# Routed experts: from adding rows in memory to writing one row per assignment and summing at the end

## The chip, the cores and the metric

One core of a Trainium2 chip runs the kernel. The metric is the device time of an execution in microseconds. A core has TensorE (PE, with its weight loads PEld), VectorE (DVE), ScalarE (ACT), GpSimd (POOL) and SyncE (SP), which run side by side and wait for one another by semaphores, and 16 DMA engines for transfers between memory and the core's own buffers.

## The reference, cut to what matters

One layer of a decoder: 512 tokens of 1024 values, float32. A mixing part (pooling, windowed attention, gates) comes first, then a mixture of experts, then a gated projection of a second input. The part at issue is the mixture:

```
x = x + merged @ w_out                                   # 512 x 1024
h2 = rmsnorm(x, g_ffn)
idx, w = route(h2, ...)                                  # 8 of 64 experts for each token, 8 weights
moe = sum over the 8: w * ((silu(h2 @ w_gate[e]) * (h2 @ w_up[e])) @ w_down[e])     # hidden width 256
x = x + moe + swiglu(h2, w_sh_gate, w_sh_up, w_sh_down)  # the shared expert
x = x + sigmoid(rmsnorm(x, g_ple) @ w_ple_gate) * rmsnorm(p @ w_ple_proj, g_ple_post)
```

512 tokens with 8 experts each are 4096 assignments, 64 for each expert on average.

## The kernel before

The kernel is one hand-ordered program: each engine has its list of instructions, and semaphores join them. Tokens are worked on in four tiles of 128 (`NT = 4`). Weights come through a ring of 12 slots of 1 MB, loaded on SyncE's queue in a written order.

**The head.** x and the input weights are loaded, ScalarE squares the rows, and then stores tile 0 of x to 128 spare "dump" rows of the accumulator in memory (L577), which only have to hold something finite. The mixing part follows. VectorE then computes the routing (L927 to L989): group scores, the best eight experts of each token, the weights, and a table `tokcol` of six columns per token and expert. TensorE counts each token's place in its expert's list (the rank product, L1469 to L1472, behind the shared expert's L1428), VectorE makes 0/1 matrices out of the places (L1002), and small products with `tokcol` (L1456) give, for each expert, a list of up to 96 tokens with their weights. VectorE turns it into row numbers (L1037 to L1046): `slot_ix` holds the token's row, and empty places point at dump rows. Meanwhile the sum of x and the shared expert's output (L1443 and L1017) is stored by ScalarE's queue as the base of the accumulator, four stores of 512 KB (L652).

**The loop over experts.** One expert is a step, on 96 rows. GpSimd gathers the rows of `h2` with an indirect DMA (L487) three steps ahead, copying the row numbers to a small buffer first (L483). TensorE transposes them (L1180), multiplies by gate and up weights (L1504, 8 products, each in two passes), transposes the activations (L1512) and multiplies by the down weights (L1525, 4 products in two passes). ScalarE evacuates half of the transposes (L659), takes the Silu (L664) and weights the result (L669); VectorE does the other half of the transposes (L1053), the product with the up part (L1058) and the transposed activations (L1063). TensorE's order in step e is: gate and up of e, transposes of e-1's activations, transposes of e+1's rows, down of e-1. GpSimd then issues an indirect DMA that adds the 96 weighted rows to the accumulator in memory (L498). Two experts may hold the same token, so each such write waits until the last has landed:

```python
pool.wait_ge(added, 16 * e)
pool.wait_ge(y_ready, e + 1)
ticket(1, ticket_done[1])
pool.indirect_dma_start(acc, ..., yrow[j][0:CAP, :], None, compute_op=ALU.add).then_inc(added, 16)
```

The row buffers `yrow` are four, so ScalarE's weighting waits for the write of four steps back. SyncE loads the three weight units of the expert four steps on, as its slots become free (L365). Further rounds for lists of more than 96 tokens exist, and are skipped with these inputs' lists.

**The tail.** When all writes have landed, GpSimd sets a marker (L564) and ScalarE's queue loads the four tiles of the accumulator back to `xrow` (L721). For each tile: ScalarE squares (L724), GpSimd takes the root (L435, L436), VectorE scales (L1137), TensorE transposes (L1180), VectorE copies with the gains (L1143), TensorE multiplies by the gate weights in two halves of 32 passes each (L1624), ScalarE takes the sigmoid (L731), VectorE multiplies and adds (L1153, L1154) and SyncE stores (L407). All the transposes of tile i+1 stand before the gate products of tile i.

Of the kernel before, what the change touches and what calls it, by code (L numbers as in the profile page):

```python
# [7 lines left out]
ALU = mybir.AluOpType  # L8
# [6 lines left out]
P = 128  # L15
# [19 lines left out]
DUMP = T  # L35
ACC_ROWS = T + P
# [4 lines left out]
UNROLL = SLOTS // 3  # L41
AHEAD = UNROLL - 1
TURNS = NE // UNROLL
NVEC = 22
LCOL = 6
# [8 lines left out]
C_NDUMP = C_P + 1  # L54
C_IC = C_NDUMP + 1
# [3 lines left out]
def constant_table():  # L59
# [10 lines left out]
    c[:, C_NDUMP] = -(DUMP + p)  # L70
# [31 lines left out]
TAIL_SLOT = [9, 10, 11, 0]  # L102

# [9 lines left out]
def build(nc, t, acc, h2_dram, out):  # L113
    ctx = ExitStack()
    with ctx:
# [3 lines left out]
        def sem(name):  # L119
# [21 lines left out]
        slot_ix = sb("slot_ix", [P, NE], U32)  # L141
        slot_w = sb("slot_w", [P, NE])
        stage = sb("stage", [P, 2, UNROLL, 1], U32)
# [29 lines left out]
        pT = qa[:, 0:1024].rearrange("p (j n) -> p j n", j=2)  # L173
        r_sc, r_sel, r_w, r_rank = (qa[:, 1024 + k * NR:1024 + (k + 1) * NR] for k in range(4))
# [4 lines left out]
        rbias = ka[:, LM + NR // 2:LM + NR // 2 + NE]  # L179
        small = ka[:, LM + NR // 2 + NE:2 * T]  # L180

        o_place = poolbuf[:, 0:NT * CAP // 2].bitcast(BF16).rearrange("p (i r) -> p i r", i=NT)
        o_iota = sb("o_iota", [P, CAP])
        o_lst = sb("o_lst", [P, LCOL + 4])
        o_ix = sb("o_ix", [P, 1], U32)
# [4 lines left out]
        hg = [xrow[:, k, :] for k in range(UNROLL)]  # L190
        yrow = [rows[:, k, :] for k in range(UNROLL)]
        hgT = [lo[:, k * KD * CAP:(k + 1) * KD * CAP].rearrange("p (k n) -> p k n", k=KD) for k in range(2)]
        eactT = [lo[:, 1536 + k * 2 * CAP:1536 + (k + 1) * 2 * CAP].rearrange("p (j n) -> p j n", j=2)
                 for k in range(2)]
# [3 lines left out]
        lists_sb = rows[:, 0, 0:NE * LCOL].rearrange("p (e c) -> p e c", c=LCOL)  # L198
        ltmp = [rows[:, 0, 512 + k * NE:512 + (k + 1) * NE] for k in range(4)]
# [3 lines left out]
        def bank(b, n=1):  # L203
# [39 lines left out]
        shdown_ps, base_ready, base_stored = (  # L243
            sem("shdown_ps"), sem("base_ready"), [sem(f"base_stored{i}") for i in range(NT)])
        dump_stored = sem("dump_stored")
# [3 lines left out]
        gathered = [sem(f"gathered{j}") for j in range(UNROLL)]  # L249
# [55 lines left out]
        def further_rounds(eng, start, step):  # L305
# [6 lines left out]
            with eng.Fori(1, ROUNDS) as j:  # L312
                with eng.If(longest > j * CAP):
                    start(j)
                    with eng.Fori(0, NE) as e:
                        step(e, (j - 1) * NE + e, j)
# [1346 lines left out]
```

## Time and profile before

| | |
|---|---|
| median of 3 runs | 1256.97 us (1254.72 to 1257.39) |
| profiled execution, span | 1254.2 us (the execution's own time is not given beside it) |
| busy: TensorE, VectorE, ScalarE, GpSimd | 1205.2, 249.3, 203.5, 256.8 us |
| mean granted clock of TensorE | 0.986 |
| moved by DMA | 288.56 MB, 230 GB/s over the span |
| chain that ended last | TensorE 90%, "issue" 5%, DMA 3%, VectorE 1%, ScalarE 1% |

The span runs from the first to the last instruction. A busy time is the sum of an engine's instructions, whether or not anybody waited for them. The granted clock is a share of TensorE's full 2.4 GHz. The chain is followed back from the last instruction, at each step to what released it; only what stands in it sets the time.

### The profile page before, as it was taken

The page shows a single profiled execution, that of the slowest core. Times are in us where ns is not written, and L with a number is a line of the kernel's source. Part 1 is how long each engine was busy: PE and PEld are TensorE (multiplying, and loading weights), DVE is VectorE, ACT ScalarE, POOL GpSimd, SP SyncE. Part 2 cuts the span into 40 slices and gives each one's busy share as a digit, 9 for nine tenths or more (in the row PEclk, how much of TensorE's full clock was granted, in tenths as well). Part 3 has the DMA queues.
Part 4 walks back from the last instruction along what each step waited for, and adds up shares of the span by engine and source line. Part 5 has one row for each costly group of instructions (what it writes and reads, how often), then busy time and mean ns, then how long its engine had stood idle before and what let it go on. Part 6 is the DMA issues. An engine that isn't in the chain of part 4 may idle for free.

```text
span 1254.2 us, 11220 instructions
## 1 busy us (share of the span) xinstructions
PE 1205.2 (96%) x3867; PEld 583.5 (47%) x3867; DVE 249.3 (20%) x525; ACT 203.5 (16%) x356; POOL 256.8 (20%) x463
## 2 busy tenths in 40 slices
PE   6999999999999899999999999999999999999498
PEld 4644544444435544444444444444444444444287
DVE  3314520121248710111011101110111011101113
ACT  2003211300130011111111111111111111111210
POOL 3261000000010113223322332233223322332100
PEclk9999999999999899999999999999999999999799
DMA  9241212114131379999999999999999999998401
GB/s 332 72 152 51 67 58 76 67 67 177 39 145 40 152 270 339 332 333 334 336 326 337 336 337 330 335 339 335 325 336 333 338 328 331 338 335 244 111 1 67
DMA packets 72154, 288.56 MB, mean 230 GB/s; under 512 B 8556, under 2 KB 30592, under 8 KB 47168
## 3 DMA queue, kind: packets, MB, share of 16 engines
q1 hardware_dynamic: 55552, 239.15, 51.1%
q0 software_dynamic: 14704, 42.25, 14.4%
q10 hardware_dynamic: 1872, 6.82, 1.4%
q8 instruction: 17, 0.28, 0.1%
q14 instruction: 9, 0.07, 0.0%
HBM read 264.58 MB, written 31.98 MB: 236 GB/s over the span
## 4 chain that ended last, share of the span: by engine, by line
PE 90%; issue 5%; DMA 3%; DVE 1%; ACT 1%; POOL 0%; SPq 0%; POOLq 0%; DVEq 0%; ACTq 0%
PE ps L1504 35%; PE ps L1525 17%; PE ps L1259 9%; PE ps L1180 5%; PE ps L1624 4%; PE ps L1361 4%; PE ps L1203 2%; PE ps L1243 2%; PE ps L1346 2%; PE ps L1344 2%; PE ps L1398 1%; DMA ring<-in_w_in 1%; PE ps L1209 1%; PE ps L1512 1%; DMA accumulator<-rows,stage 1%
## 5 line engine op out<-in xcount | busy, mean ns | idle before, releaser
L1504 PE MATMUL ps<-ring,gates 128*96 128x512 f32 x1024 | 451.7, 594 | 1.5 <-ACT gates L659 1.5
L1504 PEld LDWEIGHTS ps<-ring,gates 128*96 128x96 f32 x1024 | 167.2, 163 | 274.5 <-issue 274.5
L1525 PE MATMUL ps<-ring,gates 128*96 128x512 f32 x512 | 230.4, 592 | 1.6 <-ACT rows L669 1.2
L1063 DVE COPY gates<-ps 128x192 f32<-128x192 f32 x64 | 22.9, 358 | 646.4 <-PE ps L1512 646.4
L1525 PEld LDWEIGHTS ps<-ring,gates 128*96 128x96 f32 x512 | 79.9, 166 | 104.2 <-issue 104.2
L478 POOL TENSOR_TENSOR tickets<-cst 128x1 f32<-128x1 f32 x125 | 23.7, 190 | 473.9 <-ACT rows L669 448.3
L1259 PE MATMUL ps<-actT,ring 128*128 128x512 f32 x256 | 112.3, 595 | 0.0
L669 ACT ACTIVATE rows<-ps,slot_w 96x1024 f32<-96x1024 f32 x64 | 71.1, 1110 | 200.7 <-DMA accumulator<-rows,stage 165.6
L498 POOL DMA_INDIRECT accumulator<-rows,stage x64 | 93.2, 1457 | 30.7 <-issue 30.7
L664 ACT ACTIVATE gates<-ps 96x256 f32<-96x256 f32 x64 | 24.3, 380 | 363.0 <-PE ps L1504 363.0
L1259 PEld LDWEIGHTS ps<-actT,ring 128*128 128x128 f32 x256 | 47.9, 190 | 59.6 <-issue 59.5
L487 POOL DMA_INDIRECT xrow<-h_rows,stage x64 | 65.7, 1027 | 35.1 <-issue 33.5
L435 POOL TENSOR_SCALAR st<-st 128x1 f32<-128x1 f32 (+1 forms) x20 | 6.6, 328 | 321.5 <-ACT rows L620 241.9
L1180 PE MATMUL ps<-cst,xrow 96*128 96x96 f32 x512 | 67.5, 275 | 3.1 <-DMA xrow<-h_rows,stage 3.1
L1180 PEld LDWEIGHTS ps<-cst,xrow 96*128 96x128 f32 x512 | 63.4, 211 | 4.4 <-issue 4.4
L483 POOL COPY stage<-slot_ix 128x1 uint32 (+1 forms) x128 | 50.7, 652 | 57.1 <-DVE slot_w L1046 53.9
L1361 PE MATMUL ps<-ring,gates 128*128 128x512 f32 x128 | 55.4, 593 | 2.1 <-DVE gates L875 2.1
L1624 PE MATMUL ps<-ring,actT 128*128 128x256 f32 x256 | 56.7, 383 | 0.0
L1624 PEld LDWEIGHTS ps<-ring,actT 128*128 128x128 f32 x256 | 49.2, 193 | 6.7
L1180 PE MATMUL ps<-cst,rows 128*128 128x128 f32 x96 | 16.5, 335 | 29.5 <-DVE rows L1137 16.1
L659 ACT ACTIVATE gates<-ps 128x384 f32<-128x384 f32 x64 | 31.4, 491 | 79.0 <-PE ps L1180 79.0
L1512 PEld LDWEIGHTS ps<-cst,gates 96*128 96x128 f32 x128 | 25.2, 197 | 31.8 <-issue 31.8
(178 smaller groups left out, 805.7 us busy)
## 6 DMA issues: line engine op xcount, KB each, us to landing
ring<-in_w_exp_gate SPq DMA_DIRECT2D x64, 1024.0 KB, 7.1
ring<-in_w_exp_up SPq DMA_DIRECT2D x64, 1024.0 KB, 11.3
ring<-in_w_exp_down SPq DMA_DIRECT2D x64, 1024.0 KB, 4.8
ring<-in_w_gate SPq DMA_DIRECT2D x8, 1024.0 KB, 9.6
ring<-in_w_in SPq DMA_DIRECT2D x5, 1024.0 KB, 14.3
ring<-in_w_out SPq DMA_DIRECT2D x4, 1024.0 KB, 4.9
ring<-in_w_ple_gate SPq DMA_DIRECT2D x4, 1024.0 KB, 12.4
accumulator<-xrow ACTq DMA_DIRECT2D x5, 512.0 KB, 4.6
```

The costliest lines, as they stand in the source:

```text
L483: nc.gpsimd.tensor_copy(stage[:, kind, j, :], slot_ix[:, bass.ds(e, 1)]).then_inc(staged, 1)
L487: pool.indirect_dma_start(hg[j][0:CAP, :], None, h2_dram, bass.IndirectOffsetOnAxis(ap=stage[0:CAP, 0, j, :], axis=0), bounds_check=T - 1, ...
L498: pool.indirect_dma_start(acc, bass.IndirectOffsetOnAxis(ap=stage[0:CAP, 1, j, :], axis=0), yrow[j][0:CAP, :], None, compute_op=ALU.add).t ...
L659: nc.scalar.activation(hgT[k][:, 4:8, :], bank(1)[:, 0:4 * CAP].rearrange("p (k n) -> p k n", k=4), ACT.Copy).then_inc(hgT_hi_ready, 1)
L669: nc.scalar.activation(yrow[j][0:CAP, :], bank(6, 2)[0:CAP, :], ACT.Copy, scale=slot_w[0:CAP, bass.ds(e, 1)]).then_inc(y_ready, 1)
L1180: last = nc.tensor.transpose(bank(b0 + half)[:, k * width:(k + 1) * width], v[0:width, 4 * half + k, :], ident[0:width, 0:width])
L1259: last = mm(bank(m % 2), w[:, k, (m % 2) * P:(m % 2 + 1) * P], actT[:, k, :], start=(k == 0), stop=(k == KD - 1))
L1361: last = mm(bank(half), gates[:, k, i * P:(i + 1) * P], w[:, k], start=(k == 0), stop=(k == KD - 1))
L1504: last = mm(bank(2 + k)[0:CAP, :], hgT[k][:, q, :], w[:, q], start=(q == 0), stop=(q == KD - 1))
L1512: last = nc.tensor.transpose(bank(4)[:, q * CAP:(q + 1) * CAP], v[:, q, :], ident[0:CAP, 0:CAP])
L1525: last = mm(bank(6 + half)[0:CAP, :], eactT[k][:, q, :], w[:, q, half * 512:(half + 1) * 512], start=(q == 0), stop=(q == 1))
L1624: last = mm(bank(half)[:, c * 256:(c + 1) * 256], actT[:, k, i * P:(i + 1) * P], w[:, k], start=(k == 0), stop=(k == KD - 1))
```

## The change

Each token gets eight rows of its own in memory (`y_dram`, 4096 rows of 4 KB, those of one token side by side), one for each of its eight experts. The routing also counts, for each token, the how-manieth of its experts an expert is (six more adds over shifted copies), and this number goes through the lists as a seventh column, so that each place of a list knows its own row: 8 x token + number. The expert loop writes its weighted rows there plainly; empty places get row number 4096, which the bounds check drops. Writes of different experts no longer wait for each other, only a row buffer waits for its own last write (one semaphore per buffer).

The base (x plus the shared expert) stays in `xrow` and is no longer stored; the store to the dump rows goes too. Gathered rows have moved to `actT`, with four buffers instead of three steps of lead. In the tail SyncE loads the eight rows of each token, four chunks of two rows (1 MB) per tile, into two buffers of four ring slots; VectorE adds them up and adds the sum to `xrow`. The transposes of the tail take `xrow` as it is, and the factor of the norm is applied as the scale of the sigmoid instead. TensorE's order in the tail is now: half a tile's gate product, the next tile's transposes, the other half.

```diff
-DUMP = T
-ACC_ROWS = T + P
+ACC_ROWS = T * TOPK
-LCOL = 6
+LCOL = 7
+Y_SLOT = [1, 5]
...
+        ysum = [ring[:, s:s + 4, :].rearrange("p u n -> p (u n)").rearrange("p (r n) -> p r n", r=TOPK)
+                for s in Y_SLOT]
...
+        y_rows = y_dram.rearrange("(i p r) n -> i p r n", p=P, r=TOPK)
...
             sp.wait_ge(ple_ps, NT)
             sp.wait_ge(shdown_ps, 2 * NT)
-            for b in base_stored:
-                sp.wait_ge(b, 16)
-            for g in gathered[:AHEAD]:
-                sp.wait_ge(g, 16)
             load_expert(3, 3, None)
...
-            sp.wait_ge(y_ps, NE - UNROLL + 1)
-            sp.wait_ge(gu_ps, NE - UNROLL + 2)
+            sp.wait_ge(gu_ps, (STEPS - 1))
+            sp.wait_ge(y_ps, (STEPS - 2))
             for c, s in enumerate(TAIL_SLOT):
                 sp.dma_start(unit_view(s, KD), ple_gate[:, :, c * 256:(c + 1) * 256]
                              ).then_inc(slot_loaded[s], 16)
+            sp.wait_ge(gu_ps, STEPS)
+            sp.wait_ge(y_ps, STEPS)
+            sp.wait_ge(experts_done, 1)
+            for i in range(NT):
+                if i >= 2:
+                    sp.wait_ge(x2_ready, i - 1)
+                for c in range(4):
+                    sp.dma_start(ysum[i % 2][:, 2 * c:2 * c + 2, :], y_rows[i][:, 2 * c:2 * c + 2, :]
+                                 ).then_inc(y_loaded[i % 2][c], 16)
...
+            def scatter(j):
+                pool.indirect_dma_start(y_dram, bass.IndirectOffsetOnAxis(ap=stage[0:CAP, 1, j, :], axis=0),
+                                        yrow[j][0:CAP, :], None, bounds_check=ACC_ROWS - 1, oob_is_err=False
+                                        ).then_inc(scattered[j], 16)
+            def move(r, j, before, first=False, last=False):
+                if not last:
+                    pool.wait_ge(hgT_ps, 2 * r + 2)
+                    stage_from(r + BUF, j)
...
+                    ticket(0, ticket_done[0])
+                    gather(j)
+                if before is not None:
+                    pool.wait_ge(scattered[j], 16 * before)
+                stage_to(r, j)
...
+                pool.wait_ge(y_ready, r + 1)
                 ticket(1, ticket_done[1])
+                scatter(j)
...
-            act.dma_start(acc[DUMP:DUMP + P, :], xrow[:, 0, :]).then_inc(dump_stored, 16)
...
-            for i in range(NT):
-                act.wait_ge(base_ready, 2 * i + 2)
-                act.dma_start(acc_rows[i], xrow[:, i, :]).then_inc(base_stored[i], 16)
...
-            for i in range(NT):
-                act.dma_start(xrow[:, i, :], acc_rows[i]).then_inc(x2_loaded[i], 16)
+            def sigmoid(i):
+                act.wait_ge(rstd3_ready, i + 1)
...
+                    nc.scalar.activation(sgate[i % 2][:, half * 512:(half + 1) * 512], bank(half), ACT.Sigmoid,
+                                         scale=st[:, 0, 8 + i:9 + i]).then_inc(sgate_ready, 1)
...
+            HEAD = NE // 2
+            for b in range(2):
+                nc.vector.memset(count_of[:, b, :, 0:HEAD], 0.0)
+            link(nc.vector.tensor_copy(count_of[:, 0, :, HEAD:], r_sel.rearrange("p (i e) -> p i e", i=NT)))
+            b, span = 0, 1
+            while span < NE:
+                link(nc.vector.tensor_tensor(count_of[:, 1 - b, :, HEAD:], count_of[:, b, :, HEAD:],
+                                             count_of[:, b, :, HEAD - span:HEAD - span + NE], ALU.add))
+                b, span = 1 - b, 2 * span
...
+            nc.vector.tensor_scalar(tokcol[:, :, :, 6], place_of, -1.0, None, ALU.add)
...
-            link(nc.vector.memset(slot_ix[:, :], DUMP))
-            link(nc.vector.tensor_tensor(slot_ix[0:CAP, :], a, b_, ALU.add))
+            link(nc.vector.tensor_tensor(row, a, b_, ALU.add))
+            nc.vector.tensor_copy(from_row[0:CAP, :], row)
+            nc.vector.scalar_tensor_tensor(to_row[0:CAP, :], row, float(TOPK), L[:, :, 6], ALU.mult, ALU.add)
...
+            def gather_sum(i, first):
+                y = ysum[i % 2]
+                turn = i // 2 + 1
+                if first:
+                    dve.wait_ge(y_loaded[i % 2][0], 16 * turn)
+                    dve.wait_ge(y_loaded[i % 2][1], 16 * turn)
+                    link(nc.vector.tensor_tensor(y[:, 0:2, :], y[:, 0:2, :], y[:, 2:4, :], ALU.add))
+                    return
+                for c in (2, 3):
+                    dve.wait_ge(y_loaded[i % 2][c], 16 * turn)
+                    link(nc.vector.tensor_tensor(y[:, 0:2, :], y[:, 0:2, :], y[:, 2 * c:2 * c + 2, :], ALU.add))
+                link(nc.vector.tensor_tensor(y[:, 0, :], y[:, 0, :], y[:, 1, :], ALU.add))
+                nc.vector.tensor_tensor(xrow[:, i, :], xrow[:, i, :], y[:, 0, :], ALU.add).then_inc(x2_ready, 1)
...
+            gather_sum(0, True)
+            gather_sum(0, False)
+            for i in range(NT):
+                if i + 1 < NT:
+                    gather_sum(i + 1, True)
+                third_T(i)
+                if i + 1 < NT:
+                    gather_sum(i + 1, False)
                 if i:
-                    third_T(i - 1)
-            third_T(NT - 1)
-            for i in range(NT):
-                result(i)
+                    result(i - 1)
+            result(NT - 1)
...
+            third_T(0)
+            for i in range(NT):
+                ple_gate_half(i, 0)
+                if i + 1 < NT:
+                    third_T(i + 1)
+                ple_gate_half(i, 1)
```

## Rows read from the trace of the kernel before

**Rows 1.** Chain of waits in the expert loop (start, length, what)
```profile
708.00 3.44 PE ps L1525 x8
711.43 6.87 PE ps L1504 x16
718.30 0.20 PE ps L1512 x2
718.50 0.89 PE ps L1180 x8
```

**Rows 2.** Busy time by stretch, loop: length, busy by engine, clock, DMA share, GB/s
```profile
700.00:800.00 100.00, 100.00 (x302) 44.42 (x301) 10.34 (x27) 17.83 (x27) 28.66 (x54) 1.00 0.96 334
```

**Rows 3.** Transfers of the whole kernel: issues, median us to landing
```profile
xrow<-h_rows,stage POOLq DMA_INDIRECT x64, 8.7
accumulator<-rows,stage POOLq DMA_INDIRECT x64, 9.8
```

**Rows 4.** Who waited for whom, 500 to 1100 us: total, times, longest
```profile
ACT rows L669 <- DMA accumulator<-rows,stage: 156.3, 50, 3.4
```

**Rows 5.** Chain of waits in the tail
```profile
1169.00 6.54 DMA accumulator<-rows,stage
...
1176.32 5.17 DMA accumulator<-rows,stage
...
1181.67 3.32 DMA xrow<-accumulator
...
1188.02 3.68 PE ps L1180 x16
...
1221.99 27.64 PE ps L1624 x128
```

**Rows 6.** Busy time by stretch, where the DMA engines are full, and one idle
```profile
8.00:12.00 4.00, 1.01 (x5) 1.02 (x6) 0.43 (x1) 2.30 (x4) 1.19 (x4) 1.00 1.05 375
405.00:407.00 2.00, 2.00 (x23) 1.41 (x22) 2.00 (x3) 0.00 (x0) 0.00 (x0) 1.00 0.97 406
1150.00:1155.00 5.00, 5.00 (x20) 2.60 (x19) 1.15 (x3) 0.87 (x2) 0.00 (x0) 1.00 1.03 275
1184.00:1186.00 2.00, 0.00 (x0) 0.00 (x0) 0.00 (x0) 0.99 (x2) 0.00 (x0) 0.50 1.06 367
1188.00:1190.00 2.00, 1.98 (x9) 1.98 (x10) 1.31 (x2) 1.18 (x3) 0.59 (x3) 0.50 0.29 119
```

**Rows 7.** Timeline of TensorE at the start (in brackets: idle before, releaser)
```profile
18.32 7.11 PE L1203 MATMUL ps<-ring,actT 128*128 128x512 f32 x16 [0.84 <-DMA ring<-in_w_in]
```

**Rows 8.** Timeline of VectorE in routing and lists
```profile
375.23 0.42 DVE L960 TENSOR_TENSOR gates<-gates,kT 128x256 f32<-128x256 f32 x1
...
381.33 0.72 DVE L980 CAST kT<-cst 128x256 bf16<-128x256 f32 x1 [0.69 <-issue]
...
387.77 0.42 DVE L991 SCALAR_TENSOR_TENSOR qT<-ps,qT 128x256 f32<-128x256 f32 x1 [2.52 <-PE ps L1472]
...
403.72 0.69 DVE L1010 TENSOR_TENSOR gates<-gates,ps 128x512 f32<-128x512 f32 x1 [1.34 <-ACT gates L647]
...
409.47 0.69 DVE L1017 TENSOR_TENSOR xrow<-xrow,ps 128x512 f32<-128x512 f32 x1 [0.82 <-PE ps L1443]
...
428.93 0.27 DVE L1041 SCALAR_TENSOR_TENSOR rows<-rows 96x64 f32<-96x64 f32 x1
```

**Rows 9.** Chain of waits at the entry into the expert loop
```profile
432.05 4.77 DMA xrow<-h_rows,stage
...
438.81 8.77 PE ps L1504 x16
```

**Rows 10.** Timeline of TensorE and SyncE's queue at the same place
```profile
428.16 5.66 PE L1443 MATMUL ps<-ring,gates 128*128 128x512 f32 x8
...
440.35 0.33 SPq L365 DMA_DIRECT2D ring<-in_w_exp_gate  x1
```

**Rows 11.** Timeline of ScalarE at the end of the loop
```profile
1172.07 1.11 ACT L669 ACTIVATE rows<-ps,slot_w 96x1024 f32<-96x1024 f32 x1 [3.89 <-PE ps L1525]
```

More of the change, by code:

```diff
@@ L501, in move @@
-            def move(e, j, first=False):
-                if not first:
-                    pool.wait_ge(hgT_ps, 2 * e)
-                stage_index(0, e + AHEAD, (j + AHEAD) % UNROLL)
-                stage_index(1, e + 1, (j + 1) % UNROLL)
-                if not first:
-                    pool.wait_ge(ticket_done[0], e)
-                pool.wait_ge(staged, 2 * e + AHEAD + 3)
-                ticket(0, ticket_done[0])
-                gather(e + AHEAD, (j + AHEAD) % UNROLL)
-                scatter(e, j, first)
+                scatter(j)
@@ L543, in o_start @@
+            for r in range(BODY):
+                move(r, r % BUF, r // BUF if r >= BUF else None, first=(r == 0))
+            with pool.Fori(1, TURNS - 1) as turn:
+                for j in range(BODY):
+                    move(turn * BODY + j, j % BUF, turn * (BODY // BUF) + j // BUF)
+            for r in range(STEPS - BODY, STEPS):
+                move(r, r % BUF, r // BUF, last=(r + BUF >= STEPS))
             def o_start(j):
-                pool.wait_ge(added, 16 * NE)
+                all_scattered(pool)
@@ L1530, in _ @@
             pe.wait_ge(base_ready, 2 * NT)
-            rows_T(0, 16, 0, None)
-            def static_uses(turn):
-                return lambda s: 16 * (USES[s] + turn + 1)
-            def step(e, j, uses, prev_uses, turn, g_next, first=False, second=False, last=False):
-                up(e, j, uses)
-                if not first:
-                    acts_T(e - 1, j - 1)
-                if not last:
-                    rows_T(e + 1, g_next, j + 1, 0)
-                if not first:
-                    down(e - 1, (j - 1) % UNROLL, prev_uses, first=second)
@@ L1563, in _, with static_uses, static_step @@
-            for e in range(NE - UNROLL, NE):
-                static_step(e)
-            acts_T(NE - 1, (NE - 1) % UNROLL)
-            down(NE - 1, (NE - 1) % UNROLL, static_uses(TURNS - 1))
+            def static_uses(group):
+                return lambda slot: 16 * (USES[slot] + group + 1)
+            def static_step(r):
+                up(r, r % GROUP, r % 2, static_uses(r // GROUP))
+                if r:
+                    acts_T(r - 1, (r - 1) % 2)
+                if r + 1 < STEPS:
+                    rows_T(r + 1, (r + 1) % BUF, (r + 1) // BUF + 1)
+                if r:
+                    down(r - 1, (r - 1) % GROUP, (r - 1) % 2, static_uses((r - 1) // GROUP),
+                         first=(r == 1))
@@ new lines, in _, with uses, uses_before_it @@
+            rows_T(None, 0, 1)
+            for r in range(BODY):
+                static_step(r)
+            with pe.Fori(1, TURNS - 1) as turn:
+                for j in range(BODY):
+                    r = turn * BODY + j
+                    def uses(slot):
+                        return (turn * (BODY // GROUP) + (USES[slot] + j // GROUP + 1)) * 16
+                    def uses_before_it(slot):
+                        return (turn * (BODY // GROUP) + (USES[slot] + (j - 1) // GROUP + 1)) * 16
+                    up(r, j % GROUP, j % 2, uses)
+                    acts_T(r - 1, (j - 1) % 2)
+                    rows_T(r + 1, (j + 1) % BUF, turn * (BODY // BUF) + ((j + 1) // BUF + 1))
+                    down(r - 1, (j - 1) % GROUP, (j - 1) % 2, uses_before_it)
@@ L1569, in o_start @@
+            for r in range(STEPS - BODY, STEPS):
+                static_step(r)
+            acts_T(STEPS - 1, (STEPS - 1) % 2)
+            down(STEPS - 1, (STEPS - 1) % GROUP, (STEPS - 1) % 2, static_uses(NGROUP - 1))
             def o_start(j):
-                pe.wait_ge(added, 16 * NE)
+                all_scattered(pe)
             def o_products(e, n, j):
```

387 lines of the change are left out of this document (177 added, 210 removed).

## The prediction

> **What bounds the kernel now.** I read the chain of waits first, then busy time by stretch, then the transfers and who waits for them. The chain in the expert loop is TensorE alone. One expert is two products, two kinds of transposes and nothing between them: 3.44 + 6.87 + 0.20 + 0.89 = 11.40 us, and the pattern repeats for all 64 experts, about 725 of 1254 us [rows 1]. In the same stretch TensorE is busy for 100 of 100 us at a granted clock of 1.00 (2.4 GHz), while the DMA engines are busy for 0.96 of the time at 334 GB/s [rows 2]. The reader is to see two resources near full, of which only one ends every wait. The accumulating write of a step takes 9.8 us from issue to landing [rows 3] and ScalarE waits 156 us for it in 50 steps [rows 4], yet nothing waits for ScalarE there: the pieces of the chain meet without a gap [rows 1]. So the loop hides the old write completely, and removing its cost there brings nothing. What the change can move lies outside the loop: the start, the entry into the loop, and the tail behind the last write.
>
> **The tail before.** The last two accumulating writes follow one another because each waits for the one before: issued at 1169.00, landed 6.54 later, then 1176.32 and 5.17. Then come a marker on GpSimd, a 512 KB load issued at 1181.67 (3.32), square, root and scaling, the first transposes at 1188.02, and TensorE is then busy to 1249.63 (1221.99 + 27.64) [rows 5]. The end is 1254.2. From the load's issue that is 72.5 us, from TensorE's last product 4.6.
>
> **Part by part.**
>
> *Start.* The 512 KB store of the dump rows (L577) goes. It shares full DMA engines (375 GB/s) [rows 6] with the input weights, for which TensorE waits 0.84 us [rows 7]. At that rate the store is 1.4 us of traffic, more than the wait, so the whole wait should go: **-0.8** (ends -0.84 and 0).
>
> *Routing.* VectorE gets two small memsets (0.15 each, an estimate below the 0.42 of 256 elements), a 256-element copy (0.4), six linked adds over 256 elements (0.42 as L960, and 0.04 between) and one cast into the list table (0.72 as L980): 0.3 + 0.4 + 6 x 0.46 + 0.72 = 4.2 us. Behind it VectorE waited 2.5 us for the rank product, which stands in TensorE's queue behind the shared expert's, so 1.7 us are left over. They run into later gaps of 1.3 and 0.8 us on VectorE, where it waits for the Silu and the shared down product [rows 8]. **0**; if that cover isn't there, +1.7.
>
> *Lists.* Before the list is announced there is one linked operation more (0.27 as L1041, and 0.03 between), 64 more elements in the copy, and a copy in place of a memset, some 0.15 together [rows 8]: **+0.45** on the path, as the first gather follows the list. The four stores of the base go; the first gather was not held by them and landed in 4.77 us [rows 9]. But SyncE is moved past the waits on these stores and on the gathers, so it issues expert 3's 3 MB when the last shared product ends (428.16 + 5.66 = 433.8) rather than at 440.35 [rows 10]. That load now meets the first gather, due at 436.8. I take **+0.3**, because the gather was issued at 432.05, before it; the other end is the landing in the loaded loop, 8.7 [rows 3], so +3.9.
>
> *Loop.* **0**. GpSimd issues a gather as before and its buffers get one step more. It newly waits for the write of four steps back, which lands in 9.8 us where 45 are there; the gather queued behind that isn't late, and TensorE, which would wait for it, has three further gathers landed. Bytes per step fall a little, which matters only if traffic paces the loop (a rival below).
>
> *Last write.* The last two writes no longer wait for each other. The last weighting ends at 1173.18 (1172.07 + 1.11) [rows 11]; ticket and issue take 0.8, so the write starts at 1174.0 instead of 1176.32. A plain row write isn't in the trace. Its nearest row is the gather of the same rows onto idle engines, 4.77 us [rows 9]; the low end is the plain 512 KB load, 3.32, the high end 6.54 [rows 5]. All is written at 1178.8 rather than 1181.5: **-2.7** (ends -4.2 and -1.0).
>
> *Tail after.* Call the first load's issue 0. Eight rows per token are 16.8 MB in 16 chunks of 1 MB, against 2 MB before. Loads of expert weights have the same 8 KB runs; alone on the engines they came at 406 GB/s [rows 6], so 2.58 us a chunk; the fixed part is 3.32 less 0.5 MB at 367 GB/s [rows 5, 6] = 1.9. Tile 0's last chunk lands at 1.9 + 4 x 2.58 = 12.2. An add of 512 elements takes 0.69 and of 256 0.42 [rows 8], or 1.05 ns per further element: 2.3 for 2048, 1.23 for 1024. Behind that chunk stand 2.3 + 1.23 + 1.23, so tile 0 is summed at 17.0, where the first transposes began at 6.4 before. They no longer wait for the root, since its factor is now applied in the sigmoid. In VectorE's queue the copy out of them stands behind tile 1's first add, which waits for tile 1's second chunk: 1.9 + 6 x 2.58 = 17.4, + 2.3 + 1.3 = **21.1** for the first gate product. TensorE has stood still by then for some 25 us, but for 8 transposes. Before, after 16 idle us, the clock was 0.50 (1.2 GHz) at this place [rows 6]. At the loop's entry, which has the same form (8 transposes, a gap, then products), the first product took 8.77 [rows 9] against 6.87 [rows 1]: **+1.9**; ends 0 and 4. From there eight halves of 6.91 (27.64/4) [rows 5] and three sets of transposes of 0.89 [rows 1] follow: 55.3 + 2.7. Per tile the chunks take 10.3 us, VectorE 2.3 + 1.3 + 7.1 + 2.8 = 13.5, TensorE 14.7: TensorE paces, with little to spare. The end behind it stays 4.6. Sum 21.1 + 1.9 + 55.3 + 2.7 + 4.6 = 85.6 against 72.5: **+13.0**.
>
> That the loads reach 406 GB/s is a number I lean on. The Trainium skill (DMA: Bandwidth & Descriptors, section Bandwidth) gives 425 GB/s for a 16 MB transfer by one core; by that, which the row's 406 stays below, the first gate product would come at 20.3, 0.8 earlier.
>
> **Sum.** -0.8 + 0 + 0.45 + 0.3 + 0 - 2.7 + 13.0 = **+10.2 us**. The profiled execution has a span of 1254.2; its own time is not given, and the median shown is 1256.97 (lowest run 1254.72), 2.8 above the span. I add the difference to the median: **1267.2**, 0.8% slower. About 0.2%, 2.5 us, can be told from no change.
>
> **Rivals.**
> *A, slow reading.* The eight rows of a token lie together, so one chunk takes 8 KB out of each 32 KB; if such reads run slower, transfers come to bound the tail. The slowest stretch with full engines is 275 GB/s (the gate weights, in short runs) [rows 6]. Chunks of 3.81 put the first gate product at 28.4, and the sum of tile 3, at 67.7, holds its transposes; the tail is 93.9, the sum +18.6, **1275.6**. For it: 16.8 MB were never read in this way. Against it: the runs are as long as the expert weights'. Chance 0.12. The Trainium skill has a rule of that kind (same page, section Latency and other measured facts: row pitches from 512 KiB up run at 207 GB/s and less); at 207 GB/s the kernel would take some 1296, an estimate from that page. No row here shows it, and its shortest pitch is far above 32 KB.
> *B, a new wait at the loop's entry.* Expert 3's load takes the engines as the first gather moves. The gather lands in 8.7 instead of 4.8 and TensorE stands 3.9 more: +13.8, **1270.8**. For it: every gather under load shows 8.7 [rows 3]. Against it: the load starts 1.8 us after the gather's issue. Chance 0.11.
> *C, the loop is paced by traffic, so faster.* A step moves 3.15 MB of weights, 0.26 gathered (4096 rows over 64) and 0.39 added (96 rows): 3.80 MB in 11.40 us = 333 GB/s, the rate of [rows 2]. Now only 0.26 is written: 3.4% less, 0.39 us a step, 23 us over 60 steps, so -13, **1244**. It decides from 0.17 us a step on (60 x 0.17 = 10.2). For it: engines 0.96 busy. Against it: TensorE has no gap and full clock, and a pass of 512 columns takes 0.429 (6.87/16) here [rows 1] as in the tail, where the engines are empty (27.64/128 = 0.216 for 256 columns) [rows 5]. Chance 0.04, and 0.03 that a part of it ends within 0.2%.
> The forecast keeps 0.70. So faster 0.04, same 0.03, slower 0.93. **Range**: the low end takes the favourable ends (last write -4.2, no loss of clock, the gather unhindered), +6.5, and 1.5 for the runs' own spread: 1262. The high end holds A and B with a little over: 1278.
>
> **What would show it.** Right: a step still 11.40 us with no gap on TensorE; DMA share in the loop below 0.96; the last write landing some 5 us after issue; the first transposes about 17 us after the first load instead of 6.4, the first gate product at 21, and from there a TensorE without gaps. Wrong: a step under 11.2 (C); gaps before the later transposes, with chunks more than 3.5 us apart (A); a first gather of over 7 us (B).

## The result, and the profile after

| | before | after |
|---|---|---|
| median on the first chip | 1255.85 us (4 runs) | 1264.47 us (1264.04 to 1265.8, 4 runs) |
| ratio | | 1.0069, 95% interval 1.0054 to 1.0083 |
| median on a second chip (e4) | 1254.16 us (17 runs) | 1264.32 us (4 runs), ratio 1.0087 (1.0069 to 1.0105) |
| span of the profiled execution | 1254.2 us | 1264.0 us |
| mean granted clock | 0.986 | 0.979 |

The change costs 8.6 us by the first comparison (6.8 to 10.4 by its interval) and 10.2 by the second (8.7 to 13.2); 10.2 was forecast. The time itself was forecast at 1267.2 us, in a range of 1262 to 1278, and came out at 1264.47: 1.6 us of the difference lie in the change, 1.1 in the time before, 1256.97 by three runs and 1255.85 with the fourth. The spans of the two profiled executions differ by 9.8. I follow the 9.8 through the trace in four pieces.

**The loop.** The chain of waits in the loop, after (start, length, what):

```profile
471.76 6.87 PE ps L1541 x16
478.62 0.20 PE ps L1548 x2
478.82 0.89 PE ps L1216 x8
```

The same pieces as in [rows 1], and the first expert product to the down product before the last takes 724.4 us here (438.50 to 1162.92) and 724.5 before (438.81 to 1163.33). Busy time by stretch:

```profile
700.00:800.00 100.00, 100.00 (x302) 44.42 (x301) 10.35 (x27) 17.69 (x27) 24.60 (x54) 1.00 0.86 327
```

Against [rows 2] the DMA share fell from 0.96 to 0.86 and GpSimd has 4 us in 100 less to do, and TensorE does not notice. The loop had no use for the DMA time that it got back.

**The last write.** The chain at the loop's end, and below it the timeline of GpSimd (both after), then the marker in the chain before:

```profile
1171.54 1.12 ACT rows L669
...
1173.55 3.54 DMA accumulator<-rows,stage
```
```profile
1168.61 0.93 POOL L507 DMA_INDIRECT accumulator<-rows,stage  x1 [0.53 <-issue]
...
1177.22 0.10 POOL L570 MEMSET tickets<- 128x1 f32 x1 [2.74 <-DMA accumulator<-rows,stage]
```
```profile
1181.54 0.11 POOL tickets L564
```

The two last writes are issued 4.9 us apart, each when its rows are weighted, and a plain row write lands in 3.54 us. From the end of the last weighting to the marker it is 4.6 us (1172.65 to 1177.22); before it was 8.4 (1173.18 to 1181.54). Compare [rows 5], where the writes took 6.54 and 5.17 one behind the other. Of the 3.8 us, 2.4 were the wait of the last write for the one before it (1173.18 to 1175.54) and 1.6 are its shorter way to landing (3.54 for 5.17); some 0.2 are lost again between.

**The tail.** Its chain after:

```profile
1179.90 14.89 DMA ring<-accumulator
...
1195.24 2.30 DVE ring L1163
...
1197.57 1.30 DVE actT L1174 x2
...
1198.91 9.42 PE ps L1657 x32
1208.33 0.88 PE ps L1216 x8
1209.22 13.82 PE ps L1657 x64
1223.03 0.88 PE ps L1216 x8
1223.92 13.82 PE ps L1657 x64
1237.73 0.88 PE ps L1216 x8
1238.62 20.74 PE ps L1657 x96
```

The chain writes the wait for transfers as one long piece, though VectorE adds while the later chunks are under way. The timeline shows what lies inside it (adds, then the first transposes, then the first gate product):

```profile
1177.40 30.27 SPq L415 DMA_DIRECT2D ring<-accumulator  x16
1184.97 2.29 DVE L1163 TENSOR_TENSOR ring<-ring 128x2048 f32<-128x2048 f32 x1 [17.70 <-DMA ring<-accumulator]
1187.41 2.29 DVE L1167 TENSOR_TENSOR ring<-ring 128x2048 f32<-128x2048 f32 x1
1189.91 2.29 DVE L1167 TENSOR_TENSOR ring<-ring 128x2048 f32<-128x2048 f32 x1 [0.20 <-DMA ring<-accumulator]
1192.24 1.22 DVE L1168 TENSOR_TENSOR ring<-ring 128x1024 f32<-128x1024 f32 x1
1193.50 1.22 DVE L1169 TENSOR_TENSOR xrow<-xrow,ring 128x1024 f32<-128x1024 f32 x1
1194.78 1.97 PE L1216 MATMUL ps<-cst,xrow 128*128 128x128 f32 x8 [23.27 <-DVE xrow L1169]
...
1198.91 9.42 PE L1657 MATMUL ps<-ring,actT 128*128 128x256 f32 x32 [2.16 <-DVE actT L1174]
```

From the first load's issue (1177.40): transposes at 17.4, the first gate product at 21.5, the end at 86.6. Before, it was 6.4 and 72.5. TensorE pays 9.42 for a half that later takes 6.91. From there the pieces above meet without a gap. In the profile before, the first 64 passes were slow too, by 0.87:

```profile
1191.70 14.69 PE ps L1624 x64
```

The loads themselves, by stretch:

```profile
1180.00:1190.00 10.00, 0.00 (x0) 0.00 (x0) 4.67 (x3) 0.00 (x0) 0.00 (x0) 0.50 1.01 427
1200.00:1202.00 2.00, 2.00 (x6) 1.62 (x5) 1.97 (x2) 0.00 (x0) 0.00 (x0) 0.50 1.01 422
```

427 and 422 GB/s at full engines, and a clock of 0.50 (1.2 GHz) for TensorE, which had stood still for 23.3 us in front of 8 transposes. By the Trainium skill (DMA: Bandwidth & Descriptors, section Bandwidth) a 16 MB transfer by one core, issued from GpSimd, reaches 425 GB/s; this trace, with 16 loads of 1 MB issued from SyncE, agrees at 422 to 427.

**The head.** TensorE at the start by the timeline, after and before, then the chain after, and one piece of the chain before:

```profile
9.64 6.71 PE L1216 MATMUL ps<-cst,rows 128*128 128x128 f32 x32 [9.64 <-DMA cst<-in_constants]
```
```profile
10.98 5.18 PE L1180 MATMUL ps<-cst,rows 128*128 128x128 f32 x24 [10.98 <-DMA cst<-in_constants]
```
```profile
16.36 6.87 PE ps L1239 x16
...
284.23 43.16 PE ps L1397 x96
...
431.92 4.63 DMA actT<-h_rows,stage
...
438.50 8.79 PE ps L1541 x16
```
```profile
286.44 41.47 PE ps L1361 x96
```

The first input product comes 2.0 us earlier (18.32 before), but 1.3 of these were there before TensorE had done anything: the constants landed at 9.64 and not at 10.98. The first expert product comes only 0.3 earlier (438.81). What lies between is one row: 96 passes of the output projection take 43.16 us here and 41.47 before. By stretch:

```profile
284.00:286.00 2.00, 1.77 (x4) 0.78 (x5) 0.18 (x1) 0.00 (x0) 0.00 (x0) 0.83 1.03 414
286.00:288.00 2.00, 2.00 (x4) 0.94 (x3) 0.00 (x0) 0.00 (x0) 0.00 (x0) 0.50 0.80 273
```

The clock fell to 0.50 for some 3 us behind a gap of 2 us on TensorE (282.1 to 284.2). The kernel before has the same gap and kept 1.00 in its profiled execution. This is not the change's doing: the code there is the same, and of the 14 executions profiled in this study five show the fall, both with the old code and with the new (after, e3, e5, e7, e12). In all five the 96 passes take 43.16 us, in the other nine 41.47.

Sum of the spans: head -0.3 (-2.0 start, +1.7 clock), loop and last weighting -0.2, last write -3.8, tail +14.1: **+9.8**. Of the head's two numbers, 1.3 of the 2.0 and all of the 1.7 differ from one execution to the next and are not the change's.

### The profile page after: what moved, and what is told of

Its sections match the earlier page's. It is cut to its first block, busy times and chain, and to the rows that moved or that the text cites. A ratio compares the mean times of both kernels' runs of the same rounds, so it can differ in the third digit from the quotient of the medians.

```text
span 1264.0 us, 11318 instructions
## 1 busy us (share of the span) xinstructions
PE 1209.1 (96%) x3867; PEld 585.3 (46%) x3867; DVE 287.0 (23%) x552; ACT 204.2 (16%) x356; POOL 232.5 (18%) x462
## 4 chain that ended last, share of the span: by engine, by line
PE 93%; issue 3%; DMA 2%; DVE 1%; ACT 0%; SPq 0%; POOL 0%; POOLq 0%; DVEq 0%
PE ps L1541 35%; PE ps L1560 17%; PE ps L1295 9%; PE ps L1216 5%; PE ps L1657 5%; PE ps L1397 5%; PE ps L1279 2%; PE ps L1464 2%; PE ps L1239 2%; PE ps L1382 2%; PE ps L1380 2%; PE ps L1434 1%; DMA ring<-accumulator 1%; PE ps L1245 1%; PE ps L1548 1%
## 5 line engine op out<-in xcount | busy, mean ns | idle before, releaser
L1541 PE MATMUL ps<-ring,gates 128*96 128x512 f32 x1024 | 451.7, 594 | 1.3 <-DVE gates L1071 1.3
L1541 PEld LDWEIGHTS ps<-ring,gates 128*96 128x96 f32 x1024 | 167.2, 163 | 274.3 <-issue 272.7
L1560 PE MATMUL ps<-ring,poolbuf 128*96 128x512 f32 x512 | 230.4, 592 | 1.6 <-ACT rows L669 1.1
L1560 PEld LDWEIGHTS ps<-ring,poolbuf 128*96 128x96 f32 x512 | 79.9, 166 | 104.1 <-issue 104.1
L669 ACT ACTIVATE rows<-ps,qT 96x1024 f32<-96x1024 f32 x64 | 71.1, 1110 | 200.0 <-PE ps L1560 200.0
L502 POOL DMA_INDIRECT actT<-h_rows,stage x64 | 65.5, 1023 | 32.9 <-issue 32.0
L1216 PE MATMUL ps<-cst,actT 96*128 96x96 f32 x512 | 67.5, 275 | 3.0 <-DMA actT<-h_rows,stage 3.0
L507 POOL DMA_INDIRECT accumulator<-rows,stage x64 | 60.9, 952 | 35.4 <-issue 35.4
L1216 PEld LDWEIGHTS ps<-cst,actT 96*128 96x128 f32 x512 | 63.4, 211 | 4.3 <-issue 4.3
L1071 DVE COPY gates<-ps 128x384 f32<-128x384 f32 x64 | 35.0, 547 | 3.1 <-PE ps L1216 3.1
```

Source lines behind the costliest of these rows:

```text
L502: pool.indirect_dma_start(hg[j][0:CAP, :], None, h2_dram, bass.IndirectOffsetOnAxis(ap=stage[0:CAP, 0, j, :], axis=0), bounds_check=T - 1, ...
L507: pool.indirect_dma_start(y_dram, bass.IndirectOffsetOnAxis(ap=stage[0:CAP, 1, j, :], axis=0), yrow[j][0:CAP, :], None, bounds_check=ACC_R ...
L669: nc.scalar.activation(yrow[j][0:CAP, :], bank(6, 2)[0:CAP, :], ACT.Copy, scale=slot_w[0:CAP, bass.ds(r, 1)]).then_inc(y_ready, 1)
L1071: nc.vector.tensor_copy(hgT[k][:, 0:4, :], bank(0)[:, 0:4 * CAP].rearrange("p (k n) -> p k n", k=4)).then_inc(hgT_lo_ready, 1)
L1216: last = nc.tensor.transpose(bank(b0 + half)[:, k * width:(k + 1) * width], v[0:width, 4 * half + k, :], ident[0:width, 0:width])
L1541: last = mm(bank(2 + k)[0:CAP, :], hgT[k][:, q, :], w[:, q], start=(q == 0), stop=(q == KD - 1))
```

## The experiments

"The tail" below is always the time from the first load's issue behind the marker to the end of the span: 72.5 before, 86.6 after.

**e4: the changed kernel again; e10: the kernel before again.** They tell how far one trace can be trusted.

> The changed kernel unchanged, on the same chip as the three others: the median again some 8 to 9 us above the kernel before (ratio 1.0069). It also shows whether the clock falls at 285 us again; if it does not, the span should be 1.7 us shorter, about 1262.3.

> The kernel before, unchanged. Its first profile had the first input product at 18.32; other executions that store the dump rows have 16.87 and 17.35. If 18.32 was a slow start, this one starts near 17 and the span is near 1253; if not, 1254.2 again.

e4: ratio 1.0087, no clock fall at 285, span 1260.7 (not 1262.3: the first input product also came at 15.4 by the chain). Tail 1174.38 to 1260.7 = 86.3. e10: first input product at 17.22, span 1251.5, tail 71.2. So the first profile of the kernel before was 2.7 us longer than this one: 0.4 by the loop's entry, 0.9 in the last writes (6.54 against 5.57 for the first of them) and 1.4 in the tail (there 13.82 instead of 14.69 for the first products, and 3.28 instead of 3.68 for the transposes). In e10 the first 64 gate passes of the tail run at full clock without any change to the code:

```profile
1189.86 13.82 PE ps L1624 x64
```

The pairs differ by 9.8 and 9.2 us, but not in the same places: from e10 to e4 it is -3.1 up to the last weighting's end (-2.9 of it by the first expert product), -2.9 for the last write and +15.2 for the tail. A span of this kernel moves by 3 to 4 us from one execution to the next, and a single pair of traces doesn't carry a difference of one or two.

**e1, e12: the store of the dump rows.** e1 puts it back into the changed kernel, e12 takes it out of the kernel before.

```diff
+            act.dma_start(spare, xrow[:, 0, :]).then_inc(dump_stored, 16)        # e1, to after
-            act.dma_start(acc[DUMP:DUMP + P, :], xrow[:, 0, :]).then_inc(dump_stored, 16)   # e12, from before
```

> The changed kernel with the one 512 KB store put back on ScalarE's queue after the first squares (into spare rows that nothing reads). By my term for the start, the first product of the input weights begins 0.8 us later than in the changed kernel (16.36 us there, 18.32 in the kernel before). The two traces differ by 1.96 at that point, so a second theory says that the whole 2.0 us come from this store; a third, that the constants' load, which landed 1.3 us earlier, varies by itself, so that nothing moves. At the end of the kernel I expect less than at the start either way: 2.2 us of lead had shrunk to 0.3 by the first expert product, with 1.7 of it lost where the clock fell at 285 us in one trace and not in the other.

> The kernel before without the store of the dump rows, nothing else changed: the start's part of the change alone. The executions so far that start without it have the first input product at 15.2 to 16.5, those with it at 16.9 to 18.3: 1.2 to 1.5 us faster, ratio 0.999. My forecast's term was 0.8. Rival: the later waits of the head take it back, ratio 1.000.

e1: 1265.44 us, ratio 1.0100 (1.0080 to 1.0119) against 1.0087 of e4 on the same chip: not to be told apart. The trace says more. The timeline of TensorE at the start of e1, and below it the same of e4:

```profile
8.88 6.49 PE L1220 MATMUL ps<-cst,rows 128*128 128x128 f32 x32 [8.88 <-DMA cst<-in_constants]
...
16.87 3.67 PE L1243 MATMUL ps<-ring,actT 128*128 128x512 f32 x8 [1.49 <-DMA ring<-in_w_in]
```
```profile
8.88 4.63 PE L1216 MATMUL ps<-cst,rows 128*128 128x128 f32 x24 [8.88 <-DMA cst<-in_constants]
...
15.21 5.32 PE L1239 MATMUL ps<-ring,actT 128*128 128x512 f32 x12
```

In both the constants landed at 8.88. With the store TensorE waits 1.49 us for the input weights, without it not at all: by the chains the first input product starts at 16.87 and at 15.37. Where the constants land at 9.9 the store costs 0.65 (17.22 in e10, 16.57 in e7), where they land at 10.0 it costs 0.9 (17.35 in e3, 16.46 in e2). In the first two traces it is 0.6, counted from the landing (7.34 and 6.72 us). So the store is worth 0.6 to 1.5, and the rest of the 2.0 between the first two traces is the landing of the constants, which varies from 8.9 to 11.0 (8.88 to 10.98 in the four executions with the store, 8.88 to 10.78 in the ten without). e12: 1252.72 us, ratio 0.9983 (0.9974 to 0.9992): 1.0 to 3.3 us faster. To leave the store out is a real part of the change, and taken alone it is a gain.

**e6: writes in order again.** Each write waits, on the previous buffer's semaphore, until the write before it has landed.

```diff
+                if not first:
+                    pool.wait_ge(scattered[(j - 1) % BUF], 16 * (before_prev(r, j)))
                 pool.wait_ge(y_ready, r + 1)
                 ticket(1, ticket_done[1])
```

> The changed kernel in which every plain row write again waits until the write before has landed. If it was the serial order that made the last write late in the kernel before (1176.32 instead of 1174.0), the tail starts some 2 us later than in the changed kernel. If it was the adding write's own slowness (6.54 and 5.17 us to landing, against 3.54 of the plain one), nothing changes: write 62, issued 4.9 us ahead of write 63, has landed by then. I expect the second: 0, and 11.40 us a step.

1265.07 us, ratio 1.0077 (1.0058 to 1.0096): by the median not to be told from the changed kernel. The chain at the loop's end, and below it two lines of the timeline, the last weighting and the ticket of write 63:

```profile
1167.05 4.50 DMA accumulator<-rows,stage
...
1172.49 3.56 DMA accumulator<-rows,stage
```
```profile
1169.98 1.11 ACT L679 ACTIVATE rows<-ps,qT 96x1024 f32<-96x1024 f32 x1 [3.83 <-PE ps L1570]
1171.76 0.19 POOL L492 TENSOR_TENSOR tickets<-cst 128x1 f32<-128x1 f32 x1 [3.59 <-DMA accumulator<-rows,stage]
```

The rows of write 63 are weighted at 1171.09, and write 62 lands at 1171.55: the ticket waits for it. From the end of the last weighting to the marker it is 5.1 us (1171.09 to 1176.19), 4.6 in the changed kernel, 8.4 before. So the order alone costs some 0.5 us, not the 0 that was expected, and the median can't show so little. The rest of the 3.8 goes with the longer landings of the kernel before: write 62 took 6.54 us there (5.3 to 6.5 in the five executions with the adding write whose chains show it) and 4.50 here, although the DMA engines were idle there when it was issued (share 0.00 from 1165 to 1169) and full here (1.02 from 1167 to 1169), and write 63 took 5.17 and 3.56. This corrects my picture of the term, in which the order was the cause and the write's speed a bound. Whether the landing is longer because the write adds, or because it carries all 96 rows and not only the filled places, was not tried apart.

**e5: half of the rows.** The tail loads and adds rows 0 to 3 of each token alone.

```diff
-                for c in range(4):
+                for c in range(2):
...
-                for c in (2, 3):
-                    dve.wait_ge(y_loaded[i % 2][c], 16 * turn)
-                    link(nc.vector.tensor_tensor(y[:, 0:2, :], y[:, 0:2, :], y[:, 2 * c:2 * c + 2, :], ALU.add))
```

> The changed kernel with 8 of the 16 chunks read in the tail: it leaves out rows 4 to 7 of every token and their two adds. Theory: only tile 0's wait before the first product stands on the path. Tile 1's second chunk lands at 1.9 + 4 x 2.5 = 11.9 after the first load's issue, the first add ends at 14.2 and the copy at 15.5, against 21.5 in the changed kernel; after that TensorE is without gaps in both. So 6.0 us shorter. Rival (transfers or VectorE's adds pace the whole tail): each tile saves two adds of 2.3 and two chunks, so 10 us or more.

1258.78 us, ratio 1.0032 (1.0021 to 1.0043). First load issued at 1176.32, span 1256.8: a tail of 80.5, 6.1 less than 86.6 (by the medians 6.3 less than e6, which ran on the same chip). The first product stands at 1192.53, 16.2 after the issue instead of 21.5 (15.5 was expected), and meets a clock that rises earlier in it (8.64 instead of 9.42). Halving transfers and half of the adds gives back the first tile's wait, 5.3 us of start and 0.8 of clock, and nothing else: the other three tiles are hidden behind TensorE.

**e2, e7, e9: what stands in front of the first gate product.** e2 lets VectorE copy tile 0's transposes out before tile 1's first add. e9 keeps TensorE at work before the first transposes with products whose result is not used; e7 does both.

```diff
             for i in range(NT):
-                if i + 1 < NT:
-                    gather_sum(i + 1, True)
-                third_T(i)
+                if i == 0:                       # e2, e7
+                    third_T(0)
+                if i + 1 < NT:
+                    gather_sum(i + 1, True)
+                if i:
+                    third_T(i)
...
+            for n in range(25):                  # e9; 26 in e7
+                mm(bank(5), ident, cst[:, 0:512], start=True, stop=True)
             third_T(0)
```

> The changed kernel, in which VectorE copies tile 0's transposes out before it makes tile 1's first add, not after. My theory: the first gate product stands behind this add alone (1194.78 + 1.97 for the transposes; the copy would end at 1197.4 to 1198.1 instead of 1198.87), so the tail gets 0.8 to 1.5 us shorter. Rival: the clock decides; product columns run at 1.2 GHz until about 1203 whatever they start at, so an earlier start gains only half of that, 0.4 to 0.7 us.

> The changed kernel with the late first add, and 26 products of constants (0.86 us each, result unused) that keep TensorE busy from its last expert product to tile 0's transposes. Theory: of the tail 1.1 us are transposes and 3.2 are product columns at the slow clock (10.15 against 6.91 in the kernel with the late add alone); both go, tail 81.4 instead of 85.7. Rival: the clock does not stay up for work of that kind, or the 26 products end too late: no gain or a loss of up to 1 us.

> The changed kernel, its order of VectorE untouched, with 25 products of constants in TensorE's gap before tile 0's transposes. In the kernel with both edits the clock stayed at 1.00 but the gain was gone, since tile 1's sum, pushed back by the late add, then held TensorE. Theory: with the add first, tile 1's sum comes 28.5 us after the first load's issue and the first half of tile 0's product now ends at 28.4, so it just fits; 2.5 us are gained (9.42 against 6.91): tail 84.1, ratio to the kernel before some 0.002 below that of the changed kernel. Rival: VectorE's sums bound the tail from there on, and the gain is under 1 us.

e2: 1263.32 us, ratio 1.0074 (1.0061 to 1.0088); tail 1175.59 to 1261.3 = 85.7. The four executions with the changed kernel's tail have 86.0 (e6), 86.3, 86.5 (e1) and 86.6, so it is 0.3 to 0.9 shorter. The product starts 1.5 us earlier (20.0 after the issue) but takes 10.15 instead of 9.42: the rival. The median is 1.0 us below that of e4 on the same chip, which is within the two intervals. e7: 1265.6 us, ratio 1.0077 (1.0062 to 1.0093), tail 1177.52 to 1264.2 = 86.7: nothing gained, though the clock stayed at 1.00 into the first half. Its timeline of TensorE:

```profile
1195.26 1.06 PE L1219 MATMUL ps<-cst,xrow 128*128 128x128 f32 x8
1197.24 7.17 PE L1660 MATMUL ps<-ring,actT 128*128 128x256 f32 x32 [0.93 <-DVE actT L1174]
1206.61 1.78 PE L1219 MATMUL ps<-cst,xrow 128*128 128x128 f32 x8 [2.20 <-DVE xrow L1169]
```

The first half ends 26.9 us after the first load's issue instead of 30.9, and then TensorE waits 2.20 us for VectorE's sum of tile 1, done at 29.1. Behind this gap the clock, 1.00 until then, falls to 0.50: the transposes take 1.78 and the next 64 passes 14.86 instead of 13.82. The next bound was 1.8 us away. e9 keeps the add first: 1262.34 us, ratio 1.0061 (1.0047 to 1.0075), tail 85.8, 0.2 to 0.8 gained instead of 2.5, and the first half takes 8.86 where e6 has 8.87 without such products, so the gain is hardly clear of chance. The size is the rival's, its reason is not: from the first gate product on TensorE is without a gap. Timeline and stretch:

```profile
1191.73 1.15 PE L1216 MATMUL ps<-cst,xrow 128*128 128x128 f32 x8 [0.19 <-DVE xrow L1169]
1195.87 8.86 PE L1657 MATMUL ps<-ring,actT 128*128 128x256 f32 x32 [3.00 <-DVE actT L1174]
```
```profile
1198.00:1200.00 2.00, 2.00 (x6) 1.64 (x5) 1.97 (x2) 0.00 (x0) 0.00 (x0) 0.51 1.00 418
```

The transposes run at full clock (1.15), then TensorE stands 3.00 us for the add and the copy, and the clock falls after all, 1.00 until 1196 and 0.51 from 1198 to 1200. In these three a gain at the first product was worth less than its length: in e2 the clock took half of it or more, in e9 nearly all, and in e7, two microseconds further on, VectorE's sum took the rest.

**e3, e8, e11: the change's other part, on the kernel before.** e3 takes the deferred norm alone. e8 is e3 without the dump store and with 15 products of constants, e11 is e8 with 12.

```diff
-                pe.wait_ge(rows3_ready, i + 1)
+                pe.wait_ge(x2_loaded[i], 16)
...
-                strided_T(rows[:, i, :], i, 2 + 2 * (i % 2), P, h3T_ps)
+                strided_T(xrow[:, i, :], i, 2 + 2 * (i % 2), P, h3T_ps)
...
-                    nc.scalar.activation(sgate[i % 2][:, half * 512:(half + 1) * 512], bank(half), ACT.Sigmoid
-                                         ).then_inc(sgate_ready, 1)
+                    if half == 0:
+                        act.wait_ge(rstd3_ready, i + 1)
+                    nc.scalar.activation(sgate[i % 2][:, half * 512:(half + 1) * 512], bank(half), ACT.Sigmoid,
+                                         scale=st[:, 0, 8 + i:9 + i]).then_inc(sgate_ready, 1)
...
+            for n in range(12):                  # e11; 15 in e8
+                mm(bank(5), ident, cst[:, 0:512], start=True, stop=True)
             for i in range(NT):
                 third_T(i)
```

> The kernel before with one part of the change alone: the tail's transposes take the accumulator's rows as they land, and the factor of the norm goes into the sigmoid's scale. Theory: in the kernel before, 3.03 us lie between the landing (1184.99) and the first transposes (1188.02), for square, root and scaling; they go, and the tail is 3.0 shorter: span about 1251.2, ratio 0.9976. Rival: TensorE is in its slow clock there and pays for an earlier start with longer work; then 1.5 us.

> The kernel before with the deferred norm, without the dump store, and with 15 such products of constants before the first transposes of the tail. Theory: tail 68.8 less 1.5 for 16 transposes at full clock (3.31 to 1.8), and 1.0 to 1.5 at the start for the store: 3.7 + 1.5 + 1.4 = 6.6 us faster than the kernel before, ratio 0.995. Rival: what the deferred norm alone showed, a tail 3.7 us shorter but a median only 1.3 lower, holds for the rest too: ratio 0.998.

> The version of e8 with 12 products of constants instead of 15. There they ended at 1185.6, when tile 0 had landed at 1183.1, so 2.4 us were lost. Theory: another 2.4 us, ratio 0.995. Rival: the landing of the last adding write varies (5.2 to 6.5 us), and with 12 products the clock falls in the gap behind them where it lands late: 1 us or less.

e3: tail 1181.73 to 1250.5 = 68.8, against 72.5 and 71.2 in the two executions of the kernel before, and 71.4 in e12, whose tail is the same code. So it is 2.4 to 3.7 us shorter, two of the three times by about 2.5. The median is 1252.81 against 1254.16, ratio 0.9993 (0.9984 to 1.0002): the interval holds no change. The wait in front of the transposes is gone, as the theory has it (landing 1185.02, first transposes 1185.06); the median gives 1.3 us where 3.0 were expected. Where the rest is stays open. e8: 1251.4 us, 0.9970 (0.9959 to 0.9981), between the two expectations; the 15 products ran 2.4 us past the landing. e11: **1249.55 us against 1255.11, ratio 0.9953** (0.9939 to 0.9966), as the theory had it. Its chain:

```profile
1186.30 1.15 PE ps L1170 x8
1187.44 13.85 PE ps L1614 x64
```

What the 12 products buy is seen in the transposes, not in the passes: the 16 transposes of tiles 0 and 1 take 3.31 us in e3 and 2.40 here (timeline), a wait for tile 1's load included, and the first gate product stands 5.6 us after the first load's issue, 6.6 in e3. The 13.85 for the first 64 passes are no gain: it is 13.82 without such products in e3, e10 and e12, and only the first profile of the kernel before shows 14.69. The tail is 67.4, 1.4 less than in e3. This kernel beats both: it keeps the adding write, takes from the change the two edits that cost nothing, and adds the products. How its 5.6 us divide among the three is known only in part: e12 alone gave 2.4 on the same chip.

## Why the prediction was right

*The loop, 0.* Right, and C is refuted: a tenth of the DMA share went away and the step stayed at 11.40.

*Start, -0.8.* Right in size: 0.6 to 0.9 where the constants land late (9.6 to 11.0), 1.5 where they land early (8.88). The reason given (the whole wait of TensorE goes) is shown by e1 beside e4; what I took for a fixed wait of 0.84 moves with the landing of the constants.

*Routing, 0.* Right. The six adds take 2.72 us for the 2.76 of my estimate, VectorE no longer waits for the rank product, its first place matrix starts at 390.33 instead of 388.89, and by the second shared product it is level again (403.74 against 403.72 in [rows 8]). The cover named was the cover.

*Lists, +0.45 and +0.3.* Both too high. From the lists' copy to their announcement VectorE takes 2.3 us after (428.11 to 430.43) and 2.2 before: the replaced operations were cheaper (0.19 and 0.22). The gather landed in 4.63 us with expert 3's load issued 1.8 behind it (433.75), 4.62 to 4.92 in the other executions of the new head whose chains I read. B is refuted.

*Last write, -2.7.* It was -3.8 in the first pair and -2.9 from e10 to e4. The plain row write took 3.54 us, and I had taken 4.77 from the gather; the low end, from the 512 KB load, was the nearer row. Against e10 this hardly shows, as its adding writes were faster (7.5 us from the last weighting to the marker, not 8.4). The reason given, that the writes no longer wait for each other, is part of it: the wait was 2.4 of the 3.8 us, and by e6 it is down to 0.5 with plain writes, even if they keep their order.

*Tail, +13.0.* It was +14.1 in the first pair and +15.2 from e10 to e4, so it was 1 to 2 us too low; the second number is the larger one because the tail before took 71.2 us in e10, not 72.5. Tile 0 is summed at 17.4 (17.0 forecast), the first gate product stands at 21.5 (21.1), the clock costs 2.5 (1.9; 2.0 to 2.5 in the four executions), then no gap, as forecast. The queue order named for the 21.1, a copy behind tile 1's first add, is in the trace as named; e2 shows that it was worth 1.5 us of start but only 0.3 to 0.9 of time. Two small slips of the prediction change nothing: its terms give 21.0 where 21.1 stands, and 425 GB/s would bring the product 0.7 earlier, not 0.8. The loads came faster than taken (2.5 us a chunk at full rate), but took longer to get there: tile 0's last chunk landed 12.5 us after the first issue, forecast 12.2. A is refuted: 422 GB/s with one chunk taking 8 KB out of each 32 KB. The row of the Trainium skill that the prediction names beside A (DMA: Bandwidth & Descriptors, section Latency and other measured facts) gives 214 GB/s as the full rate of its copies, so its 207 is hardly a loss, and the 1296 us worked out from it are no price of slow reading.

The errors of one sign and the other (-0.75 lists and gather, -1.1 write, +1.1 tail, -1.2 start, +1.7 clock) nearly cancel. The forecast of 10.2 against 9.8 in the spans is therefore better than its terms, and that is luck: the fall of the clock at 285 us and the early landing of the constants, 1.7 and 1.3 us with opposite signs, were not in the prediction and are not the change's. What was right without luck is the mechanism: nothing in the loop, one write's time at its end, and the first tile's load and sum in front of a TensorE without gaps.

## What to carry to other kernels

A cost that is large in the list of waits (156 us for the adding writes) can be worth 3 to 4 us, if the waiting engine is not the one that ends the chain; what its removal buys is then the one instance that stands at the end of the loop. Moving a sum out of a loop that hides it into a tail costs the first tile's load and sum in full, here 11 us for 4 MB and five adds, however well the rest overlaps. And where TensorE meets its work at the slow clock, a microsecond gained in front of it can be worth half or less: 1.5 us of start were 0.3 to 0.9 of time in e2.

## What the runs showed of the hardware

Behind the same gap of 2.1 us on TensorE at 285 us the clock fell to 0.50 in 5 of 14 executions and stayed at 1.00 in 9, at a cost of 1.7 us where it fell. In the tail it fell behind a gap of 3.00 us in e9 and behind one of 2.20 in e7, and did not behind one of 0.93 in e7. Writes that add took 5.2 to 6.5 us to landing near the loop's end and a tenth more of the DMA engines' time in the loop than plain ones, which also leave out the empty places. How much of the tenth is the adding and how much the fewer rows was not tried apart, but the queue of GpSimd's transfers gives an estimate (packets, MB, share of the engines' time; before, then after):

```profile
q0 software_dynamic: 14704, 42.25, 14.4%
```
```profile
q0 software_dynamic: 14704, 33.87, 7.6%
```

That is 181 us of the 16 engines' time before and 96 after. At the time per byte of the kernel after, 42.25 MB would have taken 120 us. So some 24 of the 85 us are the fewer bytes and some 61 the adding, an estimate which takes gathers and plain writes to cost the same per byte.

An indirect DMA that adds keeps GpSimd for 1.43 to 1.46 us, a plain one for 0.93 to 0.95.
